# Softmax probabilities of a head pair: half divided on GpSimd and transposed, half turned by matmuls with a diagonal

## The reference, cut to what matters

```
def one(qblk):
    s = jnp.einsum("bqkgd,btkd->bkgqt", qblk, k).astype(F32) * scale
    p = jax.nn.softmax(s, axis=-1).astype(v.dtype)
    return jnp.einsum("bkgqt,btkd->bqkgd", p, v)
```

## Time and profile before

| | |
|---|---|
| median of 3 runs | 2177.48 us (2177.27 to 2179.65) |
| the profiled execution | 2177.39 us, its span 2175.8 us |
| TensorE busy | 2050.3 us, 94% of the span |
| VectorE, ScalarE, GpSimd busy | 1040.6, 538.9, 53.6 us |
| mean granted TensorE clock | 0.964 |
| the attention's pairs | from about 188 to 282 us |

### The profile page before, as it was taken

The page is one execution under the profiler, slowest core; times in us unless marked ns, Lnnn a source line. Parts: engine busy times, 40 slices in busy tenths (PEclk is TensorE's granted clock), DMA queues, the critical chain, the costliest instruction groups (busy, mean ns, idle before and its releaser), DMA issues.

```text
span 2175.8 us, 32014 instructions
## 1 busy us (share of the span) xinstructions
PE 2050.3 (94%) x13251; PEld 1842.8 (85%) x13251; DVE 1040.6 (48%) x1677; ACT 538.9 (25%) x719; POOL 53.6 (2%) x100
## 2 busy tenths in 40 slices
PE   5999988798999999998999999999998999999997
PEld 3997865488999999998859859869768999999997
DVE  5276548786225224326527337327438325324335
ACT  2325413313221221122313212212212321221221
POOL 0001200000000000000000000000000000000000
PEclk8899979898999999999999999999998999999998
DMA  8220014433443343332312212213202222222211
GB/s 256 83 80 1 2 38 157 122 96 117 120 131 97 116 154 97 97 106 88 106 39 87 78 39 91 74 39 106 77 21 78 59 77 75 74 67 76 78 58 49
DMA packets 213538, 185.30 MB, mean 85 GB/s; under 512 B 10866, under 2 KB 198706, under 8 KB 213426
## 3 DMA queue, kind: packets, MB, share of 16 engines
q1 hardware_dynamic: 209504, 172.27, 25.7%
q0 software_dynamic: 3616, 11.29, 1.6%
q10 hardware_dynamic: 305, 0.10, 0.0%
HBM read 176.42 MB, written 7.21 MB: 84 GB/s over the span
## 4 chain that ended last, share of the span: by engine, by line
PE 86%; DVE 9%; ACT 2%; issue 1%; DMA 0%; POOL 0%; DVEq 0%; SPq 0%; ACTq 0%
PE acc L524 60%; PE acc L870 4%; PE acc L896 3%; PE acc L911 3%; PE acc L550 2%; PE acc L710 2%; PE mix L579 2%; PE acc L537 2%; PE mix L887 1%; PE acc L774 1%; PE mix L680 1%; PE mix L870 1%; PE acc L699 1%; PE mix L594 1%; DVE h_lo L1356 1%
## 5 line engine op out<-in xcount | busy, mean ns | idle before, releaser
L524 PE MATMUL acc<-h_hi,w_hi 128*128 128x320 f32 x2144 | 495.6, 312 | 25.5 <-DVE h_lo L1356 6.3
L524 PE MATMUL acc<-h_lo,w_hi 128*128 128x320 f32 x2144 | 490.3, 310 | 0.0
L524 PE MATMUL acc<-h_hi,w_lo 128*128 128x320 f32 x2144 | 490.0, 310 | 0.0
L524 PEld LDWEIGHTS acc<-h_hi,w_hi 128*128 128x128 f32 x2144 | 358.1, 189 | 41.4 <-issue 33.9
L968 ACT ACTIVATE w_hi<-raw 128x2048 fp32r<-128x2048 f32 x112 | 214.3, 1914 | 694.9 <-PE acc L524 638.9
L1284 DVE TENSOR_TENSOR w_lo<-raw,w_hi 128x2048 fp32r<-128x2048 f32 x112 | 256.7, 2292 | 251.1 <-ACT w_hi L968 247.2
L524 PEld LDWEIGHTS acc<-h_lo,w_hi 128*128 128x128 f32 x2144 | 360.2, 189 | 0.0
L524 PEld LDWEIGHTS acc<-h_hi,w_lo 128*128 128x128 f32 x2144 | 360.2, 189 | 0.0
L1690 DVE TENSOR_TENSOR gu<-silu_g,acc 128x640 f32<-128x640 f32 x44 | 36.1, 821 | 416.6 <-PE acc L524 407.8
L1378 DVE SCALAR_TENSOR_TENSOR xT<-acc,mod,xT 128x128 f32<-128x128 f32 (+2 forms) x288 | 109.0, 434 | 137.2 <-PE acc L524 135.2
L524 PE MATMUL acc<-gu_hi,w_hi 128*128 128x320 f32 x704 | 160.7, 309 | 0.7 <-DVE gu_lo L1699 0.7
(11 more groups left out here) (289 smaller groups left out, 2380.8 us busy)
## 6 DMA issues: line engine op xcount, KB each, us to landing
raw<-in_l_w_in_dram SPq DMA_DIRECT2D x64, 512.0 KB, 4.4
ada_raw<-in_l_w_ada_dram SPq DMA_DIRECT2D x52, 512.0 KB, 4.5
raw<-in_l_w_gate_dram SPq DMA_DIRECT2D x44, 512.0 KB, 4.1
raw<-in_l_w_up_dram SPq DMA_DIRECT2D x44, 512.0 KB, 5.4
raw<-in_l_w_ada_dram SPq DMA_DIRECT2D x34, 512.0 KB, 4.6
raw<-in_l_w_down_dram SPq DMA_DIRECT2D x32, 512.0 KB, 4.5
raw<-in_l_w_out_dram SPq DMA_DIRECT2D x24, 512.0 KB, 4.7
raw<-in_l_w_down_dram SPq DMA_DIRECT2D x16, 384.0 KB, 3.8
```

What stands on the lines that cost most here:

```text
L524: last = mm(acc[:, 2 * r + b, 0:HALF], w[:, k * cols + col:k * cols + col + P], x[:, k, b * HALF:(b + 1) * HALF], start=(k == 0 and n == 0 ...
```

## The change

Of each pair, GpSimd multiplies the first head's probabilities in place by 1/sum (new signal `scaled`), and TensorE turns them by transposes with the identity. The second head keeps its diagonal; there are two diagonal buffers now, one for each pair in flight.

```diff
-    "rrec_ready diag_ready": "a unit's 1/sum; the same on a diagonal",
+    "rrec_ready scaled diag_ready": "a unit's 1/sum; the first head's probabilities times it; the second's 1/sum on a diagonal",
...
-        rdiag = sb("rdiag", [P, 4, P])
+        rdiag = sb("rdiag", [P, 2, P])
...
-                for g in range(2):
-                    eng.wait_ge(S["diag_ready"], 2 * p + g + 1)
-                    for m in range(1 if t == 0 else 4):
-                        last = mm(acc[:, g, m * P:(m + 1) * P], probs[:, p % 2, g, m * P:(m + 1) * P],
-                                  rdiag[:, (2 * p + g) % 4, :], start=True, stop=True)
-                    last.then_inc(S["pT_made"], pe.up("pT_made"))
+                eng.wait_ge(S["scaled"], p + 1)
+                for m in range(1 if t == 0 else 4):
+                    last = eng.transpose(acc[:, 0, m * P:(m + 1) * P], probs[:, p % 2, 0, m * P:(m + 1) * P], ident[:, :])
+                last.then_inc(S["pT_made"], pe.up("pT_made"))
+                eng.wait_ge(S["diag_ready"], p + 1)
+                for m in range(1 if t == 0 else 4):
+                    last = mm(acc[:, 1, m * P:(m + 1) * P], probs[:, p % 2, 1, m * P:(m + 1) * P], rdiag[:, p % 2, :],
+                              start=True, stop=True)
+                last.then_inc(S["pT_made"], pe.up("pT_made"))
                 if t:
-                    for g in range(2):
-                        last = mm(acc[:, 2, g * P:(g + 1) * P], probs[:, p % 2, g, 4 * P:], rdiag[:, (2 * p + g) % 4, :],
-                                  start=True, stop=True)
+                    eng.transpose(acc[:, 2, 0:P], probs[:, p % 2, 0, 4 * P:], ident[:, :])
+                    last = mm(acc[:, 2, P:2 * P], probs[:, p % 2, 1, 4 * P:], rdiag[:, p % 2, :], start=True, stop=True)
                     last.then_inc(S["pT_made"], pe.up("pT_made"))
...
             for p in range(NP):
-                for g in range(2):
-                    u = (2 * p + g) % 4
-                    if p >= 2:
-                        eng.wait_ge(S["pT_made"], turned(p - 1))
-                    eng.wait_ge(S["rrec_ready"], 2 * p + g + 1)
-                    ins = eng.tensor_scalar(rdiag[:, u, :], ident[:, :], rrec[:, u:u + 1], None, ALU.mult)
-                    ins.then_inc(S["diag_ready"], po.up("diag_ready"))
+                n, u = (N_CTX if pairs[p][0] == 0 else N), 2 * p % 4
+                eng.wait_ge(S["rrec_ready"], 2 * p + 1)
+                ins = eng.tensor_scalar(probs[:, p % 2, 0, 0:n], probs[:, p % 2, 0, 0:n], rrec[:, u:u + 1], None, ALU.mult)
+                ins.then_inc(S["scaled"], po.up("scaled"))
+                if p >= 2:
+                    eng.wait_ge(S["pT_made"], turned(p - 1))
+                eng.wait_ge(S["rrec_ready"], 2 * p + 2)
+                ins = eng.tensor_scalar(rdiag[:, p % 2, :], ident[:, :], rrec[:, u + 1:u + 2], None, ALU.mult)
+                ins.then_inc(S["diag_ready"], po.up("diag_ready"))
```

## The result

The change makes the kernel a little slower: 2184.32 us against 2177.22 us (medians of 8 runs each), ratio 1.0039 with a 95% interval of 1.0028 to 1.0051. The forecast was 2168.3 us. The time is also outside the range, by 0.3 us. The profiled execution took 2190.24 us, its span is 2188.7 us. In rows of after and of the runs, L numbers are lines of that kernel; the product helper is L524 or L525, as a line stands ahead of it.

What follows compares the result with a forecast made beforehand. TensorE bounded each latent pair; with the change a loop through GpSimd would take 4.35 us. 14 x (4.95 - 4.35) + 0.67 = 9.1 us off 2177.39 gives 2168.3 us, range 2166 to 2184.

Steps and rivals of the forecast that it cites:

- TensorE is the bound per pair: Latent attention pairs: TensorE busy all the time; five transposes save 0.67 us, its period falling from 4.95 to 4.28 us.
- The rival that transposes are not cheaper: Latent pairs: a transpose behind a product costs what the product does; period stays 4.95, time 2177.4 us; chance 0.03.
- X = 1.33: GpSimd's in-place multiplication of 128 x 640 probabilities takes 1.33 us, from a memset's slope of 1.4 ns an element.
- The bounds of 1.03 and 3.01: Range for GpSimd's multiplication: 1.03 us at ScalarE's exponential rate, 3.01 us if all time grows with the elements.
- above 2 us: Sign that the forecast is wrong: GpSimd's row for the 128 x 640 multiplication is longer than 2 us.
- The loop is 3.02 + X: Latent pairs: turn, copies, reciprocals, GpSimd, next turn take 3.02 us plus GpSimd's multiplication, 4.35 us in all.
- Forecast (X below 1.67): 0.64: Chance 0.64 that GpSimd's multiplication takes under 1.67 us and the kernel gets faster, to 2168.3 us.
- rival 1: GpSimd eats the gain in the latent pairs: multiplication of 1.67 to 2.29 us, about no change, 2177.4 us; chance 0.13.
- The ends of the stretch: First latent turn saves 0.67 us in full; the last pair's 0.15 us and the prompt's pairs are counted as nothing.
- What is gained here is therefore kept.: Behind the attention: loads issue as slots come free, the only transfer wait is 11.8 us once, so no gain is lost.
- The clock: Granted clock expected at 1.00 (2.4 GHz) from 205 us to the end of the pairs, despite the transposes.
- the third rival: The clock falls in the pairs: at 0.50 in all 14, 50 us lost, 2228 us; chance 0.03.

Runs made afterwards that it cites:

- without GpSimd's length: Changed kernel with GpSimd multiplying only the first 128 of the 640 probabilities, so the attention is not the reference's: 2175.02 us, ratio 0.9985.
- the second trace of before: The kernel before the change, run again unchanged for a second trace: 2178.22 us, ratio 1.0002.
- the two traces of after: The changed kernel's first run and its unchanged repeat: 2184.32 us (ratio 1.0039) and 2186.53 us (1.0045).
- After at before's own position: Changed kernel plus 168 semaphore increments placed where TensorE idles, putting the retention loop's code where the unchanged kernel has it: 2178.83 us, ratio 1.0017.
- After at a good position: Changed kernel plus 32 semaphore increments at TensorE's start, which move its later code and compute nothing: 2175.46 us, ratio 0.9987.
- before at a good one: Unchanged kernel plus 120 semaphore increments placed where TensorE idles (60, 25, and 5 in each of seven heads): 2171.75 us, ratio 0.9965.
- with 88: Unchanged kernel plus 88 semaphore increments at TensorE's start, which also hold the first matmul back to 14.65 us: 2181.44 us, ratio 1.0015.
- with 168 at the start: Changed kernel plus 168 semaphore increments at TensorE's start, delaying its first matmul to 26.86 us: 2192.31 us, ratio 1.0069.

## Why the prediction was wrong, point by point

- **TensorE is the bound per pair, and a turn becomes 0.67 us cheaper.** Nearly right: without GpSimd's length the pair took 4.33 us where 4.28 was forecast, a saving of 0.62 in place of 0.67. The rival that transposes are not cheaper is out: four of them took 0.59 us, four products 0.89.
- **GpSimd, X = 1.33.** This is the first step that failed, a term that was mis-sized: X is 1.89. The bounds of 1.03 and 3.01 held it, and so did the sign "above 2 us", which therefore said nothing; the other sign, a chain through GpSimd and VectorE, came. But the value was taken from the slope of a memset (1.4 ns an element), which only writes; this operation reads and writes and took 2.50. The Trainium skill's 2.6 cycles for two inputs (GPSIMD Engine Reference, section 3.1), from which the prediction had estimated X = 1.71, was nearer than the memset. The 2.50 ns measured are 3.0 cycles at that page's 1.2 GHz, so the trace lies above the page's figure too. The prediction gave the page's value as the near end of a rival only; its own value should have been nearer to it.
- **The loop is 3.02 + X.** Right, and this is why the size of X settles the pairs: 3.02 + 1.89 = 4.91, measured 4.91. TensorE's wait for the scaled probabilities was forecast at under 0.1 us a pair; it was 0.31. Where the prediction says "Forecast (X below 1.67): 0.64", rival 1 happened in the pairs: by the prediction's own sum X = 1.89 leaves 14 x 0.04 + 0.67 = 1.2 us.
- **The ends of the stretch.** "I count nothing" for the last pair. GpSimd there starts as before, with no scores on TensorE to cover it: by the same rows 275.98 + 1.89 + 0.59 + 0.04 + 1.10 = 279.60, 0.4 after the 279.19 of before. And the first period was 5.40 us (207.97 to 213.37), half a microsecond more than the later ones, because the two parts of its turn took 1.05 and 1.20 us where later turns took 0.66 and 1.10. The clock there was 0.50 until 209.5 us, which the second trace of before shows too, so this half microsecond does not belong to the change. These two take most of the 1.2 us, hence 75.81 against 75.80; that they agree so closely is luck.
- **"What is gained here is therefore kept."** This is the second step that failed: with the clock (below) it turned no gain into a loss. I looked for what a shorter attention could collide with, and found no load. But the edit also takes 168 instructions out of TensorE's program, and that moved the head of the retention loop to a position with a second wait at each jump. The price is 3.6 and 4.2 us in the two traces of after. No rival had this mechanism. The trace of before held a hint in its row of three "issue" waits at L524, 3.6 us, which I had not read.
- **The clock.** Right but for the first latent pair, and the third rival is out. The clock was 0.50 in that pair, in both traces of after and in the second of before, and 1.00 from then to the end of the pairs, with half of the turns as transposes. The Trainium skill's rule that transposes don't count as work for the clock (TensorE: Matmul & The Clock Gate, Part 4: PE-mode transpose) shows no effect in this stretch; here the scores, the values and the other turns stand between the transposes.

The sum after minus before is +7.1 us in the first comparison and 9.1 in the second. The latent pairs are 0, the position 3.6 to 4.2. Some 3 to 5 us are left. What is left lies in stretches where the clock changes (the start, the prompt's pairs, behind the attention), and there two traces of one program differ by as much. After at before's own position is 1.8 us slower (ratio 1.0017, 1.0004 to 1.0030), of which 0.9 is still at the three jumps, so the position is not the whole loss. After at a good position (0.9987) is 0.22%, 4.8 us, behind before at a good one (0.9965); those two ran on different chips, each against before on its own.

The mean granted clock of each execution tells more than two traces. In 97 executions of the three kernels with before's arithmetic (before, with 88 and with 120 increments) it is never under 0.960. In 41 of the four with the change's (after, with 32, with 168 at the start, with 168 placed) it is under 0.960 in 15, and with the heads' order turned in 3 of 24. Of the 12 of after at before's position, the seven with 0.961 or more took 2175.33 to 2179.93 us, the five with 0.960 or less 2182.88 to 2187.93 us. So the lower clock comes in some executions of the changed kernel and in none of the unchanged one: that part of the loss is not chance alone. The traces show no one place for it: behind the attention the first of after (0.957) has 34 us at 0.50 in one piece, its second (0.959) and that of after with 32 (0.958) have 10 us. Where and why the change brings the lower clock about stays open.

## What to carry to other kernels

An engine that comes off the critical path by 0.4 us has that to give and no more: before an operation on it is made five times larger, its rate has to be known from an operation of the same kind, and if it is not, the order should be chosen so that the long piece lies beside other work (here the same operations in the other order give 7.5 us in place of nothing). A change that alters the number of instructions of an engine with loops can move the time by several microseconds through the loops' position alone. Before a difference of 0.2 to 0.4% is credited to an edit, run both kernels at two or three positions, and compare the granted clocks of all their executions.

## What the runs showed of the hardware that was not expected

- TensorE's cost of a jump back depends on where the loop's head lies in its program: no wait with 32 instructions more in after, one, of 1.2 and 1.3 us on average in the two traces, at each jump in before, two of together 2.2 and 2.4 us in after.
- A multiplication by one scalar a partition on GpSimd in float32 took 0.605 us for 128 and 1.886 us for 640 elements a partition.
- A semaphore increment on TensorE at the program's start took 0.16 us (168 of them in 26.86 us).
- The same program meets the granted clock's changes at other moments in each execution. For this kernel that is 7.6 us in one stretch between two traces.
